# Attention values in plain float32, with each branch's turned bank taken by an engine of its own

## The reference, cut to what matters

```
p_cmp = softmax(q @ kc.T * scale, blocks that have ended)    # 31 compressed blocks
o_cmp = p_cmp @ vc
p     = softmax(q @ ks.T * scale, causal)                    # selected blocks: all of them at 512 tokens
o_slc = p @ vs
p     = softmax(q @ kw.T * scale, causal)                    # window of 512: all of it here
o_win = p @ vw
out   = g[0] * o_cmp + g[1] * o_slc + g[2] * o_win
```

## Time and profile before

| | us |
|---|---|
| time, median of 3 runs | 1833.69 (1833.57 to 1836.84) |
| the profiled execution, its own time | 1839.77 |
| its span | 1837.9 |
| mean granted TensorE clock, share of full | 0.993 |
| TensorE busy | 1793.4 (98%) |
| VectorE busy | 877.6 (48%) |
| ScalarE busy | 615.0 (33%) |
| attention loop, about | 541 to 668 |

### The profile page before, as it was taken

One profiled execution on the slowest core, in us unless ns is written; L12 is line 12 of the kernel. 1 busy time (PEld: TensorE's weight loads), 2 busy tenths in 40 slices (PEclk: granted clock), 3 DMA queues, 4 the chain that ended last, 5 costly groups with the idle time before them and its releaser, 6 DMA issues.

```text
span 1837.9 us, 22546 instructions
## 1 busy us (share of the span) xinstructions
PE 1793.4 (98%) x8308; PEld 1480.0 (81%) x8308; DVE 877.6 (48%) x1135; ACT 615.0 (33%) x894; POOL 105.2 (6%) x93
## 2 busy tenths in 40 slices
PE   8999999999988899999999999999999999999999
PEld 6888888877767777888888888888888878888887
DVE  5544443366777755444443344444432554444322
ACT  5333332234345644333232232333222432333211
POOL 0500000122010001000000000000000110000000
PEclk9999999999998999999999999999999999999999
DMA  5333333324310003333343323333332223333331
GB/s 173 92 103 91 102 110 96 89 82 101 84 57 13 0 19 89 99 92 102 91 122 101 98 80 93 101 91 103 116 100 64 75 81 92 102 91 114 103 102 48
DMA packets 321363, 163.70 MB, mean 89 GB/s; under 512 B 13893, under 2 KB 320041, under 8 KB 321322
## 3 DMA queue, kind: packets, MB, share of 16 engines
q1 hardware_dynamic: 321130, 163.08, 30.8%
q10 hardware_dynamic: 192, 0.08, 0.0%
HBM read 161.04 MB, written 2.10 MB: 89 GB/s over the span
## 4 chain that ended last, share of the span: by engine, by line
PE 90%; DVE 6%; ACT 2%; issue 1%; DMA 0%; SPq 0%; DVEq 0%; POOL 0%; ACTq 0%
PE ps_s L541 19%; PE ps_s L543 19%; PE ps_s L542 19%; PE ps_y L541 9%; PE ps_y L543 9%; PE ps_y L542 9%; DVE w_lo L1411 1%; PE ps_aux L541 1%; DVE pt_b L1801 1%; DVE xg_lo L1429 1%; ACT scratch L1281 1%; PE ps_aux L542 1%; PE ps_aux L543 1%; ACT w_hi L1021 1%; DVE small L1759 0%
## 5 line engine op out<-in xcount | busy, mean ns | idle before, releaser
L1411 DVE TENSOR_TENSOR w_lo<-raw,w_hi 128x1024 fp32r<-128x1024 f32 (+2 forms) x279 | 367.6, 1318 | 735.1 <-ACT w_hi L1021 734.6
L541 PE MATMUL ps_s<-xg_hi,w_hi 128*128 128x512 f32 x1608 | 632.1, 393 | 8.0 <-DVE xg_lo L1429 5.6
L543 PE MATMUL ps_s<-xg_hi,w_lo 128*128 128x512 f32 x1608 | 626.4, 390 | 0.0
L542 PE MATMUL ps_s<-xg_lo,w_hi 128*128 128x512 f32 x1608 | 626.2, 389 | 0.0
L1021 ACT CAST w_hi<-raw 128x1024 fp32r<-128x1024 f32 (+2 forms) x279 | 312.1, 1119 | 596.7 <-PE ps_s L543 302.7
L541 PEld LDWEIGHTS ps_s<-xg_hi,w_hi 128*128 128x128 f32 x1608 | 302.1, 188 | 77.3 <-DVE xg_lo L1429 8.3
L542 PEld LDWEIGHTS ps_s<-xg_lo,w_hi 128*128 128x128 f32 x1608 | 302.2, 188 | 64.2 <-issue 2.4
L543 PEld LDWEIGHTS ps_s<-xg_hi,w_lo 128*128 128x128 f32 x1608 | 302.1, 188 | 63.4
L541 PE MATMUL ps_y<-act_hi,w_hi 128*128 128x512 f32 x704 | 274.3, 390 | 0.7 <-DVE w_lo L1411 0.7
L543 PE MATMUL ps_y<-act_hi,w_lo 128*128 128x512 f32 x704 | 273.9, 389 | 0.0
L542 PE MATMUL ps_y<-act_lo,w_hi 128*128 128x512 f32 x704 | 273.9, 389 | 0.0
(11 more groups left out here) (326 smaller groups left out, 1189.7 us busy)
## 6 DMA issues: line engine op xcount, KB each, us to landing
raw<-in_ffn_w_gate SPq DMA_DIRECT2D x88, 512.0 KB, 3.9
raw<-in_ffn_w_up SPq DMA_DIRECT2D x88, 512.0 KB, 3.9
raw<-in_ffn_w_down SPq DMA_DIRECT2D x64, 704.0 KB, 4.6
raw<-in_hyb_w_in SPq DMA_DIRECT2D x19, 512.0 KB, 3.8
x_in<-in_x SPq DMA_DIRECT2D x8, 256.0 KB, 6.1
raw<-in_hyb_cmp_w SPq DMA_DIRECT2D x4, 512.0 KB, 4.0
raw<-in_hyb_w_in SPq DMA_DIRECT2D x8, 256.0 KB, 3.3
raw<-in_hyb_w_out SPq DMA_DIRECT2D x16, 128.0 KB, 2.9
```

The source lines that it names most:

```text
L541: mm(bank, hi, x_hi, start=first, stop=False, **kw)
L542: mm(bank, hi, x_lo, start=False, stop=False, **kw)
L543: return mm(bank, lo, x_hi, start=False, stop=last, **kw)
L1411: tt(w_lo[:, n % 2, 0:size], raw[:, n % 4, 0:size], f32(w_hi[:, n % 2, 0:size]), ALU.subtract).then_inc(lo_ready, 1)
```

## The change

The values (`v_t`, `vc_t`) and the turned probabilities (`pt_even`, `pt_odd`, `ptc`) are kept whole, in plain float32, and `values` issues one plain float32 product in place of `three`. Of a turned s, ScalarE copies branch 0 and VectorE branch 1, each with its own semaphore (`pt_by_act`, `pt_by_dve`); `turn` waits for each ahead of its branch and signals after each, so `pt_done` counts two per s. Everything is done at the same place in each engine's order as its predecessor. `values` also waits for `o_lo_ready`. The compressed turned bank and the values are taken by ScalarE alone. GpSimd zeroes two regions rather than four. `pt_even` and `pt_odd` lie in the memory of `pt_b`, which is still used earlier for blocks.

```diff
-                at_least(pe, pt_lo_ready, 8 * j + s)
                 for br in range(2):
+                    at_least(pe, pt_by_dve if br else pt_by_act, 8 * j + s)
                     for k in range(c + 1):
                         at = br * T + k * P
                         t = nc.tensor.transpose(ps_y[:, br, k * P:(k + 1) * P], prob_of(s)[:, at:at + P], ident)
-                t.then_inc(pt_done, 1)
+                    t.then_inc(pt_done, 1)
...
-                pe.wait_ge(pt_lo_ready, 8 * j + 2 * pair + 2)
+                pe.wait_ge(pt_by_act, 8 * j + 2 * pair + 2)
+                pe.wait_ge(pt_by_dve, 8 * j + 2 * pair + 2)
...
-                three(bank, vc_hi[:, :], vc_lo[:, :], ptc[:, 0, queries], ptc[:, 1, queries], True, False)
+                at_least(pe, o_lo_ready, 4 * j + pair)
+                mm(bank, vc_t[:, :], ptc[:, queries], start=True, stop=False)
                 for br in range(2):
                     for k in range(2 * half_pair + 2):
-                        at = (br * 4 + k) * 2 * P
-                        last_mm = three(bank, v_hi[:, br, k * P:(k + 1) * P], v_lo[:, br, k * P:(k + 1) * P],
-                                        p_hi[:, at:at + 2 * P], p_lo[:, at:at + 2 * P],
-                                        False, br == 1 and k == 2 * half_pair + 1)
+                        last_mm = mm(bank, v_t[:, br, k * P:(k + 1) * P], probs[:, br, k, :, :], start=False,
+                                     stop=br == 1 and k == 2 * half_pair + 1)
...
-            def split_values(br):
+            def take_values(br):
                 act.wait_ge(aux_done, AUX.index("t_vs") + br + 1)
-                copy(v_hi[:, br, :], ps_aux[:, :]).then_inc(v_hi_ready, 1)
+                copy(v_t[:, br, :], ps_aux[:, :]).then_inc(aux_free, 1)
...
-                copy(ptc[:, 0, :], ps_stat[0:NCP, :]).then_inc(c_pt_hi_ready, 1)
+                copy(ptc[:, :], ps_stat[0:NCP, :]).then_inc(c_pt_ready, 1)
...
-                act.wait_ge(pt_done, 8 * j + s + 1)
-                p_hi = turned_parts(pair % 2)[0].rearrange("p (b k h q) -> p b k h q", b=2, k=4, h=2)
-                copy(p_hi[:, :, 0:c + 1, c % 2, :],
-                     ps_y[:, :, 0:(c + 1) * P].rearrange("p b (k q) -> p b k q", q=P)).then_inc(pt_hi_ready, 1)
+                act.wait_ge(pt_done, 16 * j + 2 * s + 1)
+                copy(turned(pair % 2)[:, 0, 0:c + 1, c % 2, :],
+                     ps_y[:, 0, 0:(c + 1) * P].rearrange("p (k q) -> p k q", q=P)).then_inc(pt_by_act, 1)
...
-            def probs_low(j, s):
+            def take_probs(j, s):
+
                 j, s = j + s // 8, s % 8
                 c, pair = s % 4, s // 2
-                dve.wait_ge(pt_hi_ready, 8 * j + s + 1)
-                p_hi, p_lo = (x.rearrange("p (b k h q) -> p b k h q", b=2, k=4, h=2)[:, :, 0:c + 1, c % 2, :]
-                              for x in turned_parts(pair % 2))
-                tt(p_lo, ps_y[:, :, 0:(c + 1) * P].rearrange("p b (k q) -> p b k q", q=P), f32(p_hi),
-                   ALU.subtract).then_inc(pt_lo_ready, 1)
+                dve.wait_ge(pt_done, 16 * j + 2 * s + 2)
+                nc.vector.tensor_copy(turned(pair % 2)[:, 1, 0:c + 1, c % 2, :],
+                                      ps_y[:, 1, 0:(c + 1) * P].rearrange("p (k q) -> p k q", q=P)).then_inc(pt_by_dve, 1)
...
-                    if s in (2, 6):
-                        probs_c_low(j, s // 4)
```

More of the change, by code:

```diff
@@ L232, in build @@
             kc_lo = mb("kc_lo", [P, 2, NCP], F32R)
[L233 to L236, removed]
+            v_t = mb("v_t", [P, 2, NQ * P])
+            vc_t = mb("vc_t", [NCP, P])
             ob_hi = mb("ob_hi", [P, 4 * T], F32R)
@@ L239, in build @@
             prob = mb("prob", [P, 2, PW])
-            pt_b = mb("pt_b", [P, 2, 4 * T], F32R)
             prob_c = mb("prob_c", [P, NQ, NCP])
-            ptc = mb("ptc", [NCP, 2, T], F32R)
+            ptc = mb("ptc", [NCP, T])
             m1 = mb("m1", [P, T])
@@ L252, in build @@
             small_c = mb("small_c", [P, 5, NQ])
+            with ExitStack() as blocks_ctx:
+                pt_b = sb("pt_b", [P, 2, 4 * T], F32R, blocks_ctx)
+            pt_even = mb("pt_even", [P, 2, 2, 2, P])
+            pt_odd = mb("pt_odd", [P, 2, 4, 2, P])
             w2_hi, w2_lo = (q_parts[:, i, 0:2 * P].rearrange("p (c d) -> p c d", c=2) for i in range(2))
@@ L351, in build @@
         c_pt_done = sem("c_pt_done")
[L352 to L355, removed]
+        c_pt_ready = sem("c_pt_ready")
+        pt_by_act = sem("pt_by_act")
+        pt_by_dve = sem("pt_by_dve")
         pv_done = sem("pv_done")
@@ L389, in head_tiles, with turned @@
             return STATS.index(name) - STATS.index("ks") + 1
[L391 to L395, removed]
+        def turned(slot_):
+            return pt_odd[:, :, :, :, :] if slot_ else pt_even[:, :, :, :, :]
         def prob_of(s):
@@ L1199, in kc_split @@
                 act.wait_ge(aux_done, AUX.index("t_vc") + 1)
-                copy(vc_hi[:, :], ps_aux[0:NCP, 0:P]).then_inc(v_hi_ready, 1)
+                copy(vc_t[:, :], ps_aux[0:NCP, 0:P]).then_inc(aux_free, 1)
             sums_high(1)
@@ L1573, in keys_low @@
                 last.then_inc(k_lo_ready, 1)
-            def values_low(br):
-                dve.wait_ge(v_hi_ready, br + 1)
-                tt(v_lo[:, br, :], ps_aux[:, :], f32(v_hi[:, br, :]), ALU.subtract).then_inc(aux_free, 1)
             def pairs_of(n, p, c):
@@ L1747, in kc_low @@
                    f32(kc_hi[:, :, :].rearrange("p a b -> p (a b)")), ALU.subtract).then_inc(kc_ready, 1)
-                dve.wait_ge(v_hi_ready, 3)
-                tt(vc_lo[:, :], ps_aux[0:NCP, 0:P], f32(vc_hi[:, :]), ALU.subtract).then_inc(aux_free, 1)
             def maxima(j, s):
@@ L1775, in scales_c @@
                 tt(small_c[:, 3, :].unsqueeze(2), small_c[:, 2, :].unsqueeze(2), gates_c, ALU.mult).then_inc(c_scale_ready, 1)
-            def probs_c_low(j, g):
-                dve.wait_ge(c_pt_hi_ready, 2 * j + g + 1)
-                tt(ptc[:, 1, :], ps_stat[0:NCP, :], f32(ptc[:, 0, :]), ALU.subtract).then_inc(c_pt_lo_ready, 1)
             def scales(j, s):
@@ L1839, in _ @@
             output_low(3, 2)
-            probs_low(3, 7)
+            take_probs(3, 7)
             output_low(3, 3)
@@ L1974, in _ @@
             for slot_ in range(2):
-                for part in turned_parts(slot_):
-                    zeros = part.rearrange("p (b k h q) -> p b k h q", b=2, k=4, h=2)[:, :, 2 * slot_ + 1, 0, :]
-                    last = tt(zeros, consts[:, 0:2 * P].rearrange("p (b q) -> p b q", b=2),
-                              consts[:, 0:2 * P].rearrange("p (b q) -> p b q", b=2), ALU.subtract)
+                zeros = turned(slot_)[:, :, 2 * slot_ + 1, 0, :]
+                last = tt(zeros, consts[:, 0:2 * P].rearrange("p (b q) -> p b q", b=2),
+                          consts[:, 0:2 * P].rearrange("p (b q) -> p b q", b=2), ALU.subtract)
             last.then_inc(probs_zeroed, 1)
```

25 lines of the change are left out of this document (11 added, 14 removed).

## The result

| | kernel before | kernel after |
|---|---|---|
| time, median | 1835.1 us (1833.57 to 1836.84) | 1822.66 us (1820.89 to 1823.76) |
| ratio, after to before | | 0.9921, 95% interval 0.9896 to 0.9945 |
| the profiled execution | 1839.77 | 1822.51 |
| its span | 1837.9 | 1820.6 |
| mean granted clock | 0.993 | 0.998 |

The change makes the kernel 0.8% faster: 12.4 us between the medians, where 18.4 were forecast. (The median before is of four executions here, the forecast's 1833.69 was of three of them.) Forecast were 1815.3 us (1811.5 to 1826): the sign and the range held, the centre was 7.4 us too low. Yet the sum made against the profiled execution, 1821.4, was only 1.1 us from its counterpart, 1822.51. The rest of the document finds what lies between these two errors.

What follows compares the result with a forecast made beforehand. TensorE, busy 98% of the span, was taken as the bound. Stops and products -10.9 us, clock -7.0 and the rest -0.5 sum to -18.4, so 1833.69 becomes 1815.3 us, range 1811.5 to 1826.

Steps and rivals of the forecast that it cites:

- the sum made against the profiled execution: Whole kernel: -10.9 - 7.0 - 0.5 = -18.4 us, taken from the profiled 1839.77, gives 1821.4 us.
- Part 1: Attention's values product: one plain float32 product for three reduced ones costs TensorE +7.4 us, compressed blocks +0.6.
- Part 2: Turned banks in the attention stage: two copies side by side end 28 stops, 21.3 us freed less 2.4 left over.
- the tail of a stop: TensorE's stops: each ended stop gives back 0.19 us beyond its idle time, 28 x 0.19 = 5.4 us.
- The 2.4 us left over: Attention halves: 8 x 0.3 us kept for scores waiting on ScalarE's exponentials and for register and semaphore gaps.
- Part 3: TensorE's clock in the attention stage: three half-clock falls go with the idle stretches ahead of them, 7.0 us gained.
- Part 4: The rest: `vc`'s bank freed earlier before the last projection's end, -0.5 us; added waits and other items 0.
- the stage holds fixed work, so I subtract the same: Final step: the 18.4 us gain is subtracted from the unprofiled median 1833.69, 6.1 below the profiled time, giving 1815.3.
- A: Rival, attention stage: the clock falls as often as now; 1826.1 us, 1822 with one fall gone; chance 0.2.
- B: Rival, attention halves: stops move to ScalarE's exponentials or VectorE's maxima and scales; 1824.7 us, chance 0.1.
- C: Rival, values blocks and scores ahead: clock stays at half with four passes, slower at 1842 us; chance 0.03.
- D: Rival, turned banks: copies don't run side by side, VectorE ends one copy later; 1818 us, chance 0.05.

Runs made afterwards that it cites:

- the two kernels with half copies: The kernel after (1822.66 us), and it with three reduced products per block of the same rounded operands, low parts left out: 1813.30 us.
- The four kernels: Full-size chain or half copies, each with three reduced or one plain product; seven halves 108.5 (an estimate), 113.24, 92.24 and 99.94 us.
- the fourth profile: The kernel before, unaltered, profiled a fourth time: 1834.33 us at clock 0.995, 6.8 us at half clock, seven halves 111.51 us.
- the kernel with three products: The kernel after with three reduced products per block, all of the same rounded operands, low parts left out: 1813.30 us, ratio 0.9877.
- the 50 timed executions: The kernel before, unaltered, timed beside the experiments: 17 average 1834.6 us at clock 0.995, 14 average 1837.8 at 0.993, seven 1845.9 at 0.988 and 0.989.

## Why the prediction was right in its mechanism, and where its centre failed

**Part 1, the plain products.** Forecast 0.434 us per block, 0.077 more than three reduced ones, +8.0 in all. Measured 0.445 and +0.090 at full clock, and 0.08 for a compressed one: 96 x 0.090 + 16 x 0.08 = 9.9 us more TensorE work. In time less of it arrives. Between the two kernels with half copies the seven halves differ by 7.7 us (99.94 less 92.24), since the one with less work has 1.1 us of new stops, and the last values, behind the halves, by 0.8 (1170.4 less 1169.6): 8.5 us. So the term was 1.9 us short as work and 0.5 as time. The halving of the 512-column slot was nearly right. The four passes of the Trainium skill ("FP8 and Floating Point Precision", TensorE Precision Notes) agree with the row of 512 columns, read from start to start: two slots of 0.43, 0.86 us, are four of 0.215. The prediction set the pair's 1.02 us beside that figure, which holds the tail too. The 0.476 us that I had worked out from their ratio to three passes is above the 0.445 of the trace, and the measurement decides.

**Part 2, the stops.** Forecast 18.9 us (21.3 less 2.4). The four kernels give 16.3 (108.5 less 92.24). Two things make the difference. With less time at half clock there is less idle time to begin with: in the fourth profile the stops on turned and compressed banks sum to 14.7 us, not 15.9. And the tail of a stop is smaller than 0.19: in the stretch from 585.45 TensorE was idle 1.77 us, and the same half without stops is 2.34 us shorter (15.44 less 13.10); four stops share the other 0.57, 0.14 each, so 28 give 3.9 rather than 5.4 (28 x 0.19 is 5.3, a slip of 0.1). The 2.4 us left over were about right for the kernel with three products (0.9 for `ptc` in the last half and the 1.1 of new stops); in the kernel after it is 0.9.

**Part 3, the clock.** What the runs show is that the falls go with the stops, not with the kind of product. With the stops and plain products the clock was 0.992 to 0.994 in eight of ten executions, without the stops and with reduced products 0.997 to 0.999 in all four, and each fall that a profile of before shows in the halves lies behind a stop. It is no rule of one stop, one fall: most stops have none. The price was close: 7.5 us (0.44 x 17.1) against 7.0. I had compared two neighbouring halves (18.43 less 15.77), though neighbours differ when nothing falls (15.44 and 15.79); the same half in two executions gives 3.0 (18.43 in the earlier trace rows less 15.45 in the fourth profile). The fall at the start stayed, as said; but its length is not fixed, 3.4 or 6.8 us from one execution of the kernel after to the next (540.28 to 550.26 is 9.98 us with 6.8 of it; another execution of the kernel after took 9.02 with 3.4), and the same two lengths stand in the profiles of before.

**Part 4.** -0.5 us for `vc` can't be told from the first turn's own scatter: it starts between 540.1 and 542.0 us in the profiles of before and between 539.3 and 540.3 in two of after. The wait in the values: 0, shown.

**Against the profiled execution** the sum was: seven halves -16.07 (of it -7.5 the clock, and -16.3 + 7.7 = -8.6 the two parts), the first three turns +0.3, the first turn -1.3, what follows -0.2: -17.3, forecast -18.4.

**The step that failed** is the one sentence behind the sum: "the stage holds fixed work, so I subtract the same". The stage does not take a fixed time. The 7.0 us of part 3 were three falls of one execution; the median of 1833.69 lay 6.1 below it, where the 50 timed executions have clocks of 0.995 and 0.996 (its own three have none on record), so by all likelihood it had fewer of them, and a fall that the median does not hold can't be saved from it. At 1834.33 us the fourth profile, nearly that median, had one fall in the halves, 3.0 us. Beginning there, part 3 is worth 3.0 instead of 7.0, 4.0 of the 7.4 us. What the kernel after is below the fourth profile without its fall is 8.8 us (1834.33 less 3.0 less 1822.51), where parts 1, 2 and 4 had 11.4: 2.6 more, from the terms above. 0.6 is the fourth profile against the median, 0.15 the kernel after's profiled execution against its own.

**What would show it**, as forecast: two instructions per block with starts 0.43 us apart per block (0.445); waits on turned banks below 4 us (none); halves of 13.9 to 14.2 (14.26 to 14.40, the last 13.87: missed by 0.1 to 0.2); granted clock 1.0 to the end of the stage (yes, but from 547); VectorE down by some 16 us in the stage (14.3: 99.09 to 84.82 between first turn and last turn of s = 7; all halves but the first and the last had about 13.0 rather than my 12.4, and have 10.9 to 11.6 rather than 10.4).

**The rivals.** A (falls as often) is out: no fall behind 547 us in either profile of the kernel after, and 0.997 or 0.998 in all eight executions. B (stops move) is out for this kernel, though with less TensorE work (one reduced product) they do move to VectorE's scales. C (half clock in the values) is out: PEclk is 1.00 in all seven halves. D costs nothing.

What stays open: why the clock falls three times in one execution of the kernel before and once in the next, with the same instructions in the same order; and where it falls in the executions of 1845 us.

## What to carry to other kernels

Before a gain read in one profiled execution is subtracted from a median, ask why the two differ. Where the difference is itself in the rows (here three stretches at half clock), take several profiles or the clock and time of each execution, and price only what the median holds. And short repeated stops of a full TensorE are worth more than their idle time: here the tails (0.14 us each) and the clock added 11 us to some 15 in the execution with three falls, and 7 in the one with one. Plain float32 products, dearer by themselves, were a fair price for taking away the step that caused the stops; three reduced products on the same short copies would be 9 us faster still, could the low parts be had without the subtraction.

## What the runs showed of the hardware

- One kernel, before, took 1832.69 to 1847.49 us in 50 executions with granted clocks of 0.996 to 0.988; in the attention, where TensorE is 12% idle at full clock anyway (13.67 busy of 15.44 us), a us at half clock costs 0.44 us.
- A VectorE copy of 128 columns from the turned bank takes 0.283 us, of 512 columns 0.684; ScalarE's 0.275 and 0.585. The durations in the forecast (0.28, 0.683, 0.586) held. The by-shape groups of the kernel after:

```profile
L1784 DVE COPY pt_odd<-ps_y 128x512 f32<-128x512 f32 x8 | 5.5, 684 | 0.2
...
L1018 ACT COPY pt_odd<-ps_y 128x512 f32<-128x512 f32 x8 | 4.7, 585 | 0.3
...
L1784 DVE COPY pt_even<-ps_y 128x128 f32<-128x128 f32 x8 | 2.3, 283 | 0.0
L1018 ACT COPY pt_even<-ps_y 128x128 f32<-128x128 f32 x8 | 2.2, 275 | 0.2 <-PE ps_y L846 0.2
```
